# Hybrid encoder layer on one core: softmax attention rebuilt, value projection reordered, output operand split by block

## The reference

```
h = LN(concat(meta, x))
h = LN(alpha*h + 0.5*SwiGLU_1(h))                    # hidden width 2816
h = LN(alpha*h + [window_attention || gla](h @ w_in) @ w_out)
h = LN(alpha*h + 0.5*SwiGLU_2(h)); return h[:, 16:]
```

```
p = softmax(concat([q @ k_band + bias, q @ k_meta, sink]))
o = p_band @ v_band + p_meta @ v_meta
```

## Time and profile before

| | us |
|---|---|
| median of 3 runs | 1124.01 (1123.48 to 1126.19) |
| the profiled execution | 1126.17 |
| its span on the core | 1124.4 |
| TensorE busy | 1033.3 (92%) |
| VectorE busy | 730.6 (65%) |
| ScalarE busy | 386.5 (34%) |
| GpSimd busy | 34.1 (3%) |

### The profile page before, as it was taken

How to read it: one execution, slowest core, us unless ns; L and a number is a source line. 1 busy time by engine, 2 the same in 40 slices (tenths; PEclk the granted TensorE clock), 3 DMA queues, 4 the chain that set the end, 5 groups by cost and what they waited for, 6 DMA issues and landing times.

```text
span 1124.4 us, 16615 instructions
## 1 busy us (share of the span) xinstructions
PE 1033.3 (92%) x6716; PEld 676.9 (60%) x6716; DVE 730.6 (65%) x1187; ACT 386.5 (34%) x492; POOL 34.1 (3%) x95
## 2 busy tenths in 40 slices
PE   3799999999899988899998988879999999989995
PEld 2588888888688875795575643334444444434443
DVE  7756665668855566757565747776666666876645
ACT  2622222225311135644235533172222223441104
POOL 1000000000000000000000000000000000000000
PEclk9799999999999998999999999989999999989998
DMA  4233232232232211121220001203323322412202
GB/s 153 70 110 112 75 112 89 97 112 103 104 104 99 68 53 38 41 72 39 75 75 1 1 1 46 98 7 113 111 76 111 112 92 94 144 62 103 103 1 75
DMA packets 25168, 88.70 MB, mean 79 GB/s; under 512 B 2859, under 2 KB 5123, under 8 KB 25123
## 3 DMA queue, kind: packets, MB, share of 16 engines
q1 hardware_dynamic: 24256, 87.24, 22.1%
q10 hardware_dynamic: 867, 0.85, 0.3%
HBM read 85.99 MB, written 2.10 MB: 78 GB/s over the span
## 4 chain that ended last, share of the span: by engine, by line
PE 75%; DVE 14%; ACT 8%; issue 2%; DMA 1%; ACTq 0%; POOL 0%; DVEq 0%
PE PS L481 34%; PE PS L517 22%; PE PS L572 7%; DVE cmax L1245 3%; DVE wsp L1267 3%; PE PS L466 2%; ACT wsp L907 2%; PE PS L816 2%; PE PS L835 2%; ACT H L901 1%; PE PS L556 1%; DVE big L1345 1%; PE PS L693 1%; DVE X L1194 1%; ACT xs L899 1%
## 5 line engine op out<-in xcount | busy, mean ns | idle before, releaser
L481 PE MATMUL PS<-xs,wsp 128*128 128x264 f16 (+1 forms) x3168 | 471.4, 312 | 13.0 <-ACT xs L899 8.4
L481 PEld LDWEIGHTS PS<-xs,wsp 128*128 128x128 f16 x3168 | 310.0, 98 | 174.4 <-issue 10.7
L907 ACT ACTIVATE wsp<-stage,wscale 128x2048 f16<-128x2048 f32 (+2 forms) x73 | 156.5, 2144 | 383.0 <-DVE wscale L1231 211.0
L1267 DVE SCALAR_TENSOR_TENSOR wsp<-stage,wscale,wsp 128x2048 f16<-128x2048 f32 (+2 forms) x73 | 184.6, 2528 | 119.2 <-ACT wsp L907 119.2
L517 PE MATMUL PS<-big,wsp 128*128 128x264 f16 (+1 forms) x1584 | 238.6, 314 | 11.7 <-DVE big L1345 9.5
L517 PEld LDWEIGHTS PS<-big,wsp 128*128 128x128 f16 x1584 | 155.5, 99 | 94.5 <-DVE big L1345 12.6
L1245 DVE TENSOR_REDUCE cmax<-stage 128x1 f32<-128x2048 f32 (+2 forms) x73 | 179.6, 2461 | 3.9
L1279 DVE SCALAR_TENSOR_TENSOR big<-PS,oscale,tmp_a 128x528 f32 (+3 forms) x44 | 33.3, 758 | 75.8 <-ACT tmp_a L914 75.8
L914 ACT ACTIVATE tmp_a<-PS,oscale 128x528 f32<-128x528 f32 (+1 forms) x44 | 30.5, 693 | 135.7 <-PE PS L481 135.7
L572 PE MATMUL PS<-xs,wsp 128*128 128x264 f16 (+1 forms) x384 | 66.5, 328 | 0.1
L1760 POOL PARTITION_ALL_REDUCE call<-cmax x73 | 30.0, 411 | 929.9 <-DVE cmax L1245 929.9
(11 more groups left out here) (169 smaller groups left out, 713.1 us busy)
## 6 DMA issues: line engine op xcount, KB each, us to landing
stage<-in_gate SPq DMA_DIRECT2D x44, 512.0 KB, 3.7
stage<-in_up SPq DMA_DIRECT2D x44, 512.0 KB, 4.5
stage<-in_down SPq DMA_DIRECT2D x32, 704.0 KB, 5.1
stage<-in_w_in SPq DMA_DIRECT2D x16, 512.0 KB, 4.6
stage<-in_w_out SPq DMA_DIRECT2D x8, 512.0 KB, 4.4
X<-in_xT SPq DMA_DIRECT2D x2, 1056.0 KB, 7.1
out_T<-H SPq DMA_DIRECT2D x8, 256.0 KB, 2.1
stage<-in_w_in SPq DMA_DIRECT2D x2, 576.0 KB, 4.3
```

The source lines that it names most:

```text
L481: return nc.tensor.matmul(dst, w, x, start=k == 0 and wp + xp == 0, stop=k == KD - 1 and xp == 1)
L907: nc.scalar.activation(wsp[:, slot, 0, 0:cols], stage[:, slot, 0:cols], ACT.Copy, scale=wscale[:, slot:slot + 1]).then_inc(w_hi, 1)
L1267: nc.vector.scalar_tensor_tensor(wsp[:, slot, 1, 0:cols], stage[:, slot, 0:cols], wscale[:, one], wsp[:, slot, 0, 0:cols], ALU.mult, ALU.s ...
```

## The change

1. **Value projection.** ScalarE makes the high part of weight chunk 3 before it copies value tile 0 out, and copies value tiles 0, 1 and 2 before the second direction's decays. VectorE's `chunk_max` of chunk 3 moves ahead of `gates(0)`, its scale between `gates(0)` and `gates(1)`, and its low part ahead of `decayed_outer(0, 0)`.
2. **End of the projections.** Softmax query tiles 1 to 3 are cut in quarters and the steps of the second GLA pair lie between these, so that all six steps are over before the key and value projections. VectorE masks the chunks 1 to 5 of the second pair back to back; `norm_step`s of head 0 come after them, those of head 1 around the chunk `OUT0`, and all six of head 2, in the loop before, come ahead of the attention. `norm_sums(2)` and `(3)` move ahead of the value projection.
3. **A bound in place of the largest value.** `gate_bound` and `value_bound` reduce the output gates and the softmax values and make from them an upper bound of `mix`; the common scale is found at unit 1 of the attention. `largest_gla`, the reductions L1656 and the last chain L1717 go.
4. **Transpositions.** `diag` and L1649 go; VectorE multiplies the row of exponentials by the reciprocal in place (`att_norm`), and TensorE transposes with the transpose operation against the identity, one instruction per piece. Three PSUM banks (4, 5, 6) take the groups in turn, `PT` has two buffers, and the values use bank 7 alone.
5. **Values.** `att_values(n-1)` is cut in two parts, which come after units 0 and 1 of block n.
6. **Output split.** The result of a block goes from PSUM straight into its high part (ScalarE, after unit 2 of the next block) and low part (VectorE); the GLA heads are split in units 12 to 15. TensorE runs the GLA half of output tile 0 before the last values and that of tile 1 after them.

```diff
@@ TensorE
+                for b, lo in enumerate([0] + [SINK_COL + 1 + BLOCK * b for b in range(len(blocks))]):
+                    mm = nc.tensor.transpose(PS[:, 4 + i % 3, b * P:(b + 1) * P], p[:, lo:lo + P], ident[:, :])
-                    mm = nc.tensor.matmul(PS[:, 4 + g, i * P:(i + 1) * P], p[:, lo:lo + P], diag[:, u % 2, g, :],
-                                          start=True, stop=True)
...
-                if UNITS[u][1] == REP - 1:
-                    att_values(UNITS[u][0])
+                n, j = UNITS[u]
+                if n and j < 2:
+                    att_values(n - 1, j)
+            out_part(0, True)
+            att_values(NB - 1, 0)
+            att_values(NB - 1, 1)
+            out_part(1, True)
+            out_part(0, False)
+            out_part(1, False)
+            for n in range(2, KD):
+                out_part(n, True)
+                out_part(n, False)
@@ TensorE, att_values(n, part)
+                    pe.wait_ge(pt_out, 2 * REP * (n + 1))
+                    if n:
+                        pe.wait_ge(m_ready, n)
+                for i in range(2) if part == 0 else range(2, len(keys)):
@@ TensorE, out_part(n, gla)
+                for k in range(REP, KD) if gla else range(REP):
+                    if n == 0 and gla:
+                        pe.wait_ge(o_lo, k - REP + 1)
+                    elif n == 0 and k == 0:
+                        pe.wait_ge(m_ready, NB)
@@ TensorE, mixer_projections
+                gla_states(1, 4)
+                proj_start(AQ + 2)
+                proj_quarter(AQ + 2, 0)
+                gla_step(1, 0)
+                proj_quarter(AQ + 2, 1)
+                gla_step(1, 1)
+                proj_quarter(AQ + 2, 2)
+                gla_step(1, 2)
+                proj_quarter(AQ + 2, 3).then_inc(proj_ready, 1)
+                norm_sums(0)
+                gla_step(1, 3)
+                proj_start(AQ + 3)
+                proj_quarter(AQ + 3, 0)
+                gla_step(1, 4)
+                proj_quarter(AQ + 3, 1)
+                norm_sums(1)
+                gla_step(1, 5)
+                proj_half(AQ + 3, 1)
+                proj_half(AK, 0)
+                norm_sums(2)
+                proj_half(AK, 1)
+                norm_sums(3)
+                proj_half(AV, 0)
+                proj_half(AV, 1)
@@ ScalarE, mixer_projections
                 proj_out(GQ + 1)
+                projection_hi(3)
+                proj_out(GV)
                 decays(0, 0)
-                proj_out(GV)
-                projection_hi(3)
                 proj_out(GV + 1)
+                proj_out(GV + 2)
                 decays(0, 1)
...
+                proj_out(AQ + 3)
+                split_hi(OUT0, OUT0 % 2, OUT_COLS)
+                norm_root(2)
+                proj_out(AK)
+                norm_root(3)
                 proj_out(AV)
@@ ScalarE, attention loop
+                n, j = UNITS[u]
+                if n and j == 2:
+                    att_out_hi(n - 1)
+                if n == NB - 1:
+                    gla_out_hi(j)
+            att_out_hi(NB - 1)
@@ VectorE, mixer_projections
                 projection_lo(2)
+                projection_max(3)
                 gates(0)
+                projection_scale(3)
                 gates(1)
                 exponents(0, 0)
                 exponents(0, 1)
-                projection_max(3)
+                projection_lo(3)
                 decayed_outer(0, 0)
-                projection_scale(3)
-                projection_lo(3)
...
                 projection_scale(8)
+                for c in range(1, NCH):
+                    mask_scores(1, c)
                 projection_lo(8)
+                for n in range(1, NORM_STEPS):
+                    norm_step(n)
                 projection_max(N_IN)
+                norm_step(NORM_STEPS + 1)
+                norm_step(NORM_STEPS + 2)
                 projection_scale(N_IN)
+                norm_step(NORM_STEPS + 3)
+                norm_step(NORM_STEPS + 4)
                 projection_lo(N_IN)
+                norm_step(2 * NORM_STEPS - 1)
+                gate_bound()
+                for n in range(2 * NORM_STEPS, 3 * NORM_STEPS):
+                    norm_step(n)
+                value_bound()
@@ VectorE, att_norm(u), in place of att_recip(u)
+                for g in range(GROUPS):
+                    i = 2 * u + g
+                    p = score_buf(i)[:, 0:unit_cols(u)]
                     dve.wait_ge(p_rec, i + 1)
-                    nc.vector.tensor_scalar(diag[:, u % 2, g, :], ident[:, :], srec[:, i:i + 1], None, ALU.mult)
+                    nc.vector.tensor_scalar(p, p, srec[:, i:i + 1], None, ALU.mult).then_inc(p_norm, 1)
@@ VectorE, attention loop
             for u in range(len(UNITS)):
                 if u + 1 < len(UNITS):
+                    att_norm(u + 1)
                 if u + 2 < len(UNITS):
                     att_max(u + 2)
+                n, j = UNITS[u]
+                if u == 1:
+                    back_scale(MIX, 1.0 / ALPHA)
+                if u < NORM_STEPS:
+                    norm_step(3 * NORM_STEPS + u)
+                if n and j == 2:
+                    att_out_lo(n - 1)
+                if n == NB - 1:
+                    gla_out_lo(j)
+            att_out_lo(NB - 1)
```

More of the change, by code:

```diff
@@ L181, in build @@
         mix = part("big", [P, KD, T])
+        sg = part("big", [P, G_HEADS, T])
+        mark_gv = pools["big"][1]
         gv = part("big", [CH, NCH, G_HEADS * DV])
-        sg = part("big", [P, G_HEADS, T])
         kT = sb("kT", [P, KEYS])
@@ L209, in build @@
         pools["X"][1] = 0
-        PT = part("X", [P, GROUPS, 4, REP * BLOCK])
+        pools["big"][1] = mark_gv
+        PT = [part(pool, [P, GROUPS, 4, REP * BLOCK]) for pool in ("X", "big")]
         rel_1 = part("arena", [P, S_MID + S_END])
         rels = (rel, rel_1)
-        diag = part("arena", [P, 2, GROUPS, P])
         gO = mix[:, REP:KD, :]
@@ L695, in outputs, with proj_quarter @@
                 mm.then_inc(o_ready, 1)
+            def proj_quarter(n, part):
+                return proj_products(n, PS[:, n % 2, 0:SEQ], (P, N_META, T), False, range(2 * part, 2 * part + 2))
             def gla_step(j, c):
@@ new lines, in out_part @@
+            def out_part(n, gla):
+                c = OUT0 + n // 2
+                if gla:
+                    pe.wait_ge(w_ready, c + 1)
+                    pe.wait_ge(res_done, KD + n + 1)
+                    if n < 2:
+                        pe.wait_ge(s_max, 2 * len(UNITS))
+                if n == KD - 1 and not gla:
+                    sum_tiles(2)
+                for k in range(REP, KD) if gla else range(REP):
[3 more added lines that the diff above has]
+                        pe.wait_ge(m_ready, NB)
+                    for wp, xp in PRODUCTS:
+                        w = w_view(c % 2, wp, KD, 2 * P)[:, k, P * (n % 2):P * (n % 2 + 1)]
+                        mm = nc.tensor.matmul(acc(1, 2 * (n % 2)), w, tokens(1, xs[:, xp, k, :]),
+                                              start=gla and k == REP and wp + xp == 0, stop=not gla and k == REP - 1 and xp == 1)
+                if not gla:
+                    mm.then_inc(res_ready, 1)
@@ L851, in _ @@
                     att_scores(u + 2)
-                if UNITS[u][1] == REP - 1:
-                    att_values(UNITS[u][0])
-            for n in range(KD):
-                c = OUT0 + n // 2
-                pe.wait_ge(w_ready, c + 1)
-                res_tile(1, KD + n, n % 2, lambda p, k: w_view(c % 2, p, KD, 2 * P)[:, k, P * (n % 2):P * (n % 2 + 1)],
-                         lambda p, k: xs[:, p, k, :], KD, m_ready if n == 0 else None, norm=2 if n == KD - 1 else None)
+                n, j = UNITS[u]
[10 more added lines that the diff above has]
+                out_part(n, False)
             layer_norm(2)
@@ L1165, in _ @@
                     att_exp(u + 2)
-            for k in range(KD):
-                act.wait_ge(h_step, 4 * MIX + 3)
-                nc.scalar.activation(xs[:, 0, k, N_META:T], mix[:, k, N_META:T], ACT.Copy, scale=hscale[:, MIX:MIX + 1]).then_inc(m_hi, 1)
+                n, j = UNITS[u]
[4 more added lines that the diff above has]
+            att_out_hi(NB - 1)
             for n in range(N_OUT):
@@ L1567, in mixer_projections @@
                 projection_scale(7)
-                norm_step(0)
                 state_step(1, 1)
@@ L1572, in mixer_projections @@
                 state_step(1, 2)
-                norm_step(NORM_STEPS)
+                norm_step(0)
                 state_step(1, 3)
@@ L1636, in att_max, with att_norm @@
                                                    accum_out=smin[:, i:i + 1]).then_inc(s_max, 1)
-            def att_recip(u):
+            def att_norm(u):
                 for g in range(GROUPS):
```

188 lines of the change are left out of this document (89 added, 99 removed).

## The result

The changed kernel takes 1098.9 us (median of 4 runs, 1098.44 to 1100.66); the kernel before, on the same chip, 1125.1 (4 runs, 1123.48 to 1130.12). The ratio is 0.976, with a 95% interval of 0.973 to 0.980. I had forecast 1109 and a range of 1099 to 1119: the direction is right, the gain is 26 us where I had 15, and the time lies just under the range.

A forecast was written before the change was run, and what follows sets the result against it. TensorE was taken as the bound in the mixer, apart from a few holes. The terms -6.3 + 4.0 - 6.4 - 6.5 - 2.1 + 2.5 = -14.8 on the profiled 1126.2 gave 1111.4, so 1109 by the median; range 1099 to 1119.

The forecast's parts named there:

- Blocks 1 and 2: Attention, second and third blocks: 33.3 us against 39.8, -6.5, with a value product at 0.93; bounds 3 and 10.
- The clock: Attention: half clock slows TensorE in block 0 and the first values, +2.5 us; bounds 0 and 8.
- Rival C: TensorE stays at 1.2 GHz all through the attention and the kernel is slower, 1152 us; chance 0.05.
- Front, -6.3: Value projection: both holes and the slow stretch behind them go, -6.3 us; bounds 0 and 6.4.
- End of the projections, +4.0: Up to the first transposition: VectorE's 25.1 us of work in a row makes it 4.0 us later; bounds 0 and +8.
- Block 0, -6.4: First attention block: transposition 4 comes 11.0 us after transposition 0, where it was 17.4; bounds 4 and 8.
- The changes of block: Attention, j = 2: VectorE waits for ScalarE's high part before normalizing the next block's first row; TensorE hole of 2.2 us.
- Block 3: Last attention block to output tile 2: -2.1 us; hole of 4.35 goes, one of 2.3 comes before tile 2.
- `att_norm` at 0.57: VectorE's in-place scaling of 401 columns taken at 0.57 us, from a range of 0.36 to 0.57.
- A: VectorE keeps up: `att_norm` at L1449's rate and no clock fall give 1103.5 us; chance 0.15.
- B: The front's gain does not come, or waits at each change of block add up: 1115 us; chance 0.20.
- D: The bound only moves the wait; the hole returns before output tile 2 in full: within 0.3% of 1124; chance 0.05.

The follow-up runs named there:

- e2: The kernel before with only the value products' order changed, the two groups alternating for each key piece: 1110.9 us, ratio 0.987.
- e5: The kernel before with the value products alternating, but both groups writing partitions 0 to 63 in two banks: 1130.2 us, ratio 1.003.
- e1: The changed kernel with the value products in each part group by group again: 1117.6 us, ratio 0.992.
- e7: The changed kernel with VectorE's low part of a block's result one unit later, behind scaling the next block's first rows: 1092.0 us, ratio 0.970.
- e3: The changed kernel with each transposition an ordinary two-instruction matmul against the identity: 1103.4 us, ratio 0.980; Rival C's number there was 1102 to 1105.
- e4: The kernel before with the value projection's reordering alone: 1117.7 us, ratio 0.993.
- e8: The changed kernel with VectorE's maximum and scale of weight chunk `OUT0+1` ahead of the last block's low part: 1096.6 us, ratio 0.973.

## Why the prediction was right in direction and too small

**The step that failed is the price of a value product in "Blocks 1 and 2": "A value product is 0.93".** That is its price in the old order. I read the loop in the diff as a split in parts and passed over its turn. In the changed kernel the six and eight products of blocks 0 and 1 take 3.16 and 4.02 where I had 5.6 and 7.5: 5.9, and that is the miss of this line (-12.5 for -6.5). In block 3 another 6.2 were there to gain (7.5 and 5.6 at 0.93; 8 x 0.50 and 2.94 at full clock), of which the clock took 2.9. `e2` and `e5` show the cause: in the turned loop the two groups' products, which go to different halves, run two at a time. Block 2 as I wrote it (4.1, 4.0, 7.5 and 2.2) adds up to 17.8 and not 17.3, so by its own terms the line was -6.1.

**The clock was mis-sized in place and amount.** I put 2.5 into block 0. There it was 0.50 from 594 to 598, where the first transposing row and the scores behind it took 1.51 and 1.28; the same work took 0.84 and 0.73 later, so it cost at most 1.2 (behind that, TensorE waits for VectorE). It fell again in block 3 behind the hole of 1.98, where eight instructions took 3.28 and 3.68 instead of 2.08 and 1.94, and cost 4.7 (11.8 us for work of 7.1). So two errors stood against each other: 12.1 us of the products' time that I did not see, and some 3 us of clock beyond my term. With the loop not turned (`e1`) the forecast of 1109 would have met a measured 1117.6: inside the range, but with a clock term about 10 too small. The sign that I had named for this, a granted clock below 0.9 past the first values, showed in both kernels.

Rival C (1.2 GHz throughout) did not occur. The Trainium skill ("TensorE: Matmul & The Clock Gate", "Part 4: PE-mode transpose") says that such transpositions don't bring the clock up as products do. In `e7` the clock is 1.00 from 600 us to beyond output tile 2, with 100 of these instructions between the other products; that they have a part in the falls of the changed kernel is not excluded by `e3`, which came out at rival C's number there, but has more work as well as shorter holes.

**Front, -6.3: right.** -6.8 by the rows, 7.5 by `e4`, both holes gone, clock 1.00.

**End of the projections, +4.0: right, by its steps.** VectorE works from 567.23 to 592.23 with 0.34 idle, 25.0 for my 25.1 (my terms add up to 25.2); the value projection stalls 1.7 for my 1.8, with 1.11 before the first scores beside it.

**Block 0, -6.4:** 11.54 for 11.0. **The changes of block:** holes of 2.21 and 1.98 for my 2.2, ended as forecast: low part at 618.70 behind ScalarE's high part, normalization at 619.55. Before output tile 2, 2.14 for 2.3, again with VectorE's order as the cause, which `e8` shows. Block 3 came out 2 shorter than forecast: its value products saved 6.2, the clock took 4.7.

**`att_norm` at 0.57: too high.** It takes 424 ns for 401 columns and 357 for 273, 0.52 ns a column with 0.22 fixed. From L1649 alone I took a small fixed part and a full column price; it was the reverse. The Trainium skill's tier table, which I had weighed and set aside ("VectorE: DVE Perf Modes", "The perf-mode tier table"), gives twice the rate, and the slope agrees. My 3 us for it would have been right only where VectorE holds the pace: in blocks 1 and 2 it does so only at the changes of block.

**Rivals A, B and D.** A's time is the nearest, and its rate for `att_norm` was right, but its reason was not the cause. B had the wrong sign. D did not occur: of 4.35 before the output projection, 2.14 come back before tile 2.

## What to carry to other kernels

When a loop around matmuls is reordered, price the new order and not the instruction: products with 64 columns of weights that go to different halves of the partitions ran two at a time here, unless a product with another number of rows stood between the two groups. Turning the loop gave 14 us on the kernel before, of 26 in all. When a matmul step is made cheaper, lay out the other engines' lists first; halving the transpositions alone gave nothing: VectorE's steps and a copy queued behind exponentials kept the pace, and the holes cost clock. And a hole on TensorE can cost more than its length, so the second reading after any gain is the granted clock behind the holes that are left.

## What the hardware showed that I had not expected

- Neighbouring float32 products of 512 columns with 64 columns of weights: 0.475 us each into alternate halves of the partitions, 0.90 alternating into the same half. One group after the other they take 0.93 to 1.0 when each group starts with a product of 16 rows, and 0.485 when all have 128 rows (1.94 for four in `e1`): value products of 16 and of 128 rows never ran side by side in these traces.
- The scaling of a float32 tile by a column in place: 285 ns for 128 columns, 357 for 273, 424 for 401, all near 0.22 us + 0.52 ns a column.
- Behind the hole of 1.98 the granted clock was 0.54, 0.50 and 0.68 for twelve microseconds in which the engine was busy without a break: 11.8 us for work of 7.1.
